# Second layer's attention stage: quartered low parts of the weight units computed by GpSimd instead of VectorE

## The reference, cut to what matters

```python
s = einsum('bnqhgd,bnkhd->bnhgqk', qb, kband) * dh ** -0.5     # 48 jobs: 4 token tiles x 12 heads
m = maximum(max(s), sink); p = exp(s - m)
p = p / (sum(p) + exp(sink - m))
o = einsum('bnhgqk,bnkhd->bqhd', p, vband)
mo = softmax(mq @ mk.T * dh ** -0.5) @ mv                       # 16 jobs: 4 tiles x 4 heads
mix = concatenate([o, mo]) @ w_out[l]
k, v = split(layer_norm(mem_2) @ w_mkv)                         # the second block's memory, for two layers
```

## Time and profile before

| | |
|---|---|
| median of 3 runs | 2278.38 us (2277.81 to 2281.79) |
| the profiled execution, its own time | 2280.4 us |
| its span | 2278.9 us |
| mean granted clock of TensorE | 0.958 |
| PE busy in the span | 2111.9 us (93%) |
| DVE busy | 1168.8 us (51%) |
| ACT busy | 883.9 us (39%) |
| POOL busy | 231.7 us (10%) |

### The profile page before, as it was taken

The page is one execution under the profiler, slowest core; times in us unless marked ns, Lnnn a source line. Parts: engine busy times, 40 slices in busy tenths (PEclk is TensorE's granted clock), DMA queues, the critical chain, the costliest instruction groups (busy, mean ns, idle before and its releaser), DMA issues.

```text
span 2278.9 us, 24588 instructions
## 1 busy us (share of the span) xinstructions
PE 2111.9 (93%) x9984; PEld 1716.7 (75%) x9984; DVE 1168.8 (51%) x2252; ACT 883.9 (39%) x1565; POOL 231.7 (10%) x155
## 2 busy tenths in 40 slices
PE   6998899999997999999999999999998899799787
PEld 6986688888786777788887878878776666577575
DVE  5325453333226666453332237998865248655553
ACT  5336443222124356442322222477451222456520
POOL 1000010000002000010000003766500000000000
PEclk9998599999998999999999999999999899999998
DMA  6330022233233212222222322322322312011211
GB/s 225 114 117 11 10 83 93 93 99 105 102 107 114 67 55 75 93 97 98 93 93 93 111 93 96 108 74 74 102 74 74 110 56 70 23 38 56 74 56 56
DMA packets 28800, 192.60 MB, mean 85 GB/s; under 512 B 3264, under 2 KB 3408, under 8 KB 7440
## 3 DMA queue, kind: packets, MB, share of 16 engines
q1 hardware_dynamic: 24848, 175.96, 22.5%
q0 software_dynamic: 3264, 12.99, 1.7%
q10 hardware_dynamic: 576, 2.10, 0.2%
HBM read 186.84 MB, written 4.19 MB: 84 GB/s over the span
## 4 chain that ended last, share of the span: by engine, by line
PE 77%; DVE 15%; ACT 6%; issue 1%; DMA 0%; POOL 0%; SPq 0%; DVEq 0%; POOLq 0%; ACTq 0%
PE bank L390 22%; PE bank L391 21%; PE bank L392 21%; DVE bank L1971 4%; PE bank L1660 2%; DVE WL L362 1%; PE bank L1551 1%; ACT WH L348 1%; PE bank L1090 1%; PE bank L1648 1%; PE bank L1099 1%; PE bank L1027 1%; PE bank L1561 1%; PE bank L2112 1%; PE bank L1653 1%
## 5 line engine op out<-in xcount | busy, mean ns | idle before, releaser
L390 PE MATMUL bank<-XH,WH 128*128 128x512 f32 (+1 forms) x1504 | 598.5, 398 | 25.4 <-DVE XL L551 10.3
L392 PE MATMUL bank<-XH,WL 128*128 128x512 f32 (+1 forms) x1504 | 568.5, 378 | 0.0
L391 PE MATMUL bank<-XL,WH 128*128 128x512 f32 (+1 forms) x1504 | 567.9, 378 | 0.0
L362 DVE TENSOR_TENSOR WL<-RAW,WH 128x2048 fp32r<-128x2048 f32 x128 | 293.2, 2291 | 462.8 <-ACT WH L348 462.8
L348 ACT ACTIVATE WH<-RAW 128x2048 fp32r<-128x2048 f32 x148 | 282.3, 1908 | 347.1 <-PE bank L392 341.7
L390 PEld LDWEIGHTS bank<-XH,WH 128*128 128x128 f32 x1504 | 286.8, 191 | 94.6 <-issue 24.7
L391 PEld LDWEIGHTS bank<-XL,WH 128*128 128x128 f32 x1504 | 287.1, 191 | 54.4 <-issue 5.6
L392 PEld LDWEIGHTS bank<-XH,WL 128*128 128x128 f32 x1504 | 286.3, 190 | 53.3 <-issue 0.6
L1971 DVE SCALAR_TENSOR_TENSOR bank<-conv_in,cols,bank 128x512 f32<-128x512 f32 x290 | 198.1, 747 | 1.1
L390 PE MATMUL bank<-WH,XH 128*128 128x512 f32 (+2 forms) x416 | 154.6, 372 | 9.8 <-DVE XL L551 6.3
L391 PE MATMUL bank<-WL,XH 128*128 128x512 f32 (+2 forms) x416 | 153.7, 369 | 0.0
(11 more groups left out here) (316 smaller groups left out, 3023.8 us busy)
## 6 DMA issues: line engine op xcount, KB each, us to landing
RAW<-weights SPq DMA_DIRECT2D x164, 1024.0 KB, 4.9
row_a<-rows POOLq DMA_DIRECT2D x7, 512.0 KB, 5.8
row_b<-rows POOLq DMA_DIRECT2D x6, 512.0 KB, 6.0
x_res<-x SPq DMA_DIRECT2D x1, 2048.0 KB, 16.7
kv<-mem_park POOLq DMA_DIRECT2D x2, 1024.0 KB, 5.1
out<-x_res ACTq DMA_DIRECT2D x4, 512.0 KB, 2.6
mem_tok<-mem SPq DMA_DIRECT2D x1, 1024.0 KB, 5.0
mem_tok<-mem POOLq DMA_DIRECT2D x1, 1024.0 KB, 8.4
```

What stands on the lines that cost most here:

```text
L362: dve.tensor_tensor(WL[j][:, :], RAW[j][:, :], WH[j][:, :].bitcast(F32), ALU.subtract).then_inc(*lo.mark())
L390: pe.matmul(ps, ah, bh, start=first, stop=False)
L391: pe.matmul(ps, ah, bl, start=False, stop=False)
L392: return pe.matmul(ps, al, bh, start=False, stop=last)
```

## The change

POOL gets a function `lower_quarter_pool`, with the body of `lower_quarter_dve` on the other engine, and `sliding_pool` runs the stage's 32 quarters in their order (`beside_pool`), with the four parking DMAs placed behind the last quarter of every second unit. `sliding_dve` issues no quarters. At the end of its stage DVE waits until U69 is lowered (`split_lo >= BESIDE_FIRST + 8`, which is 70). POOL begins with a wait for DVE's last lowering before the stage. `split_lo` counts in order, so each side waits for the other at the two seams.

```diff
+    def lower_quarter_pool(q):
+        u, j = lowered_pool[0], lowered_pool[0] % 2
+        s = slice(q * UNIT // 4, (q + 1) * UNIT // 4)
+        last = q == 3
+        if last:
+            POOL.wait_ge("split_hi", u + 1)
+        else:
+            POOL.wait_ge(*after("quarter", u, q))
+        part = pool.tensor_tensor(WL[j][:, s], RAW[j][:, s], WH[j][:, s].bitcast(F32), ALU.subtract)
+        part.then_inc(*(lo.mark() if last else G.mark()))
+        lowered_pool[0] += last
...
+    BESIDE_FIRST = U["mem2_kv", 0, 0] + 2
...
-    def beside_dve(e):
-        if e in QUARTERS:
-            lower_quarter_dve(QUARTERS[e])
-
-    def park_pool():
-        for layer in range(2):
-            POOL.wait_ge(*after("emptied", U["mem2_kv", layer, 1], 1))
-            pool.dma_start(mem_park[layer][:, 0:1024], m2_keys[:, :]).then_inc(*parked_keys.mark("park", layer, "keys", by=16))
-            POOL.wait_ge(*after("emptied", "mem2_v", layer, MEMT - 1))
-            pool.dma_start(mem_park[layer][:, 1024:2048], m2_values[:, :]).then_inc(*parked_values.mark("park", layer, "values", by=16))
+    def beside_pool():
+
+        lowered_pool[0] = BESIDE_FIRST
+        POOL.wait_ge("split_lo", BESIDE_FIRST)
+        for e in range(BESIDE_ENTRIES):
+            if e not in QUARTERS:
+                continue
+            lower_quarter_pool(QUARTERS[e])
+            if QUARTERS[e] == 3:
+                layer, unit = divmod(lowered_pool[0] - BESIDE_FIRST - 1, 4)
+                if unit == 1:
+                    POOL.wait_ge(*after("emptied", U["mem2_kv", layer, 1], 1))
+                    pool.dma_start(mem_park[layer][:, 0:1024], m2_keys[:, :]).then_inc(*parked_keys.mark("park", layer, "keys", by=16))
+                elif unit == 3:
+                    POOL.wait_ge(*after("emptied", "mem2_v", layer, MEMT - 1))
+                    pool.dma_start(mem_park[layer][:, 1024:2048], m2_values[:, :]).then_inc(
+                        *parked_values.mark("park", layer, "values", by=16))
+        lowered_pool[0] = U[A_SLOTS[2]]
...
-            for other in beside(n, BESIDE_LAGS[1]):
-                beside_dve(other)
             if n % 3 == 2 and n < 12:
                 rotate_dve(q_tok, SH - KB, ("q", 1), KB, ("q", 1), range(n // 3, n // 3 + 1), LATE_BLOCKS[0])
+        lowered[0] = BESIDE_FIRST + 8
+        DVE.wait_ge("split_lo", BESIDE_FIRST + 8)
...
-        park_pool()
+        beside_pool()
```

## The result

| | before | after |
|---|---|---|
| median of 13 runs each | 2277.81 us (2272.06 to 2281.79) | 2291.07 us (2280.92 to 2293.62) |
| ratio after / before | | 1.0055, 95% interval 1.0038 to 1.0072 |
| the profiled execution | 2280.4 us | 2293.11 us |
| its span | 2278.9 us | 2291.7 us |
| mean granted clock | 0.958 | 0.956 |

The account below looks back on a forecast made before the run. PE was taken to set the stage's pace. Stage -0.3 us (-0.3 - 0.3 + 0.3) and the seam summed to +0.6 us: 2281.0 for the profiled execution, median 2279.0, range 2276.5 to 2283.0.

Parts of the forecast that it names:

- Where PE waits for a quarter: At PE's starts of U64 and U67: POOL's later last quarters add 0.3 us and 0.0 or 0.1 us.
- DVE's held operations beside POOL: Stage's DVE operations with two SBUF inputs: line 1605 held at worst 1.29 us, within about 1.5 us slack; nothing charged.
- the wait of line 1607: PE's wait around 840 us for a small DVE operation behind a quarter: goes with the quarter, -0.3 us.
- rival B: Clock, at the stage's end: the new halt in the transposes delays full clock into the projection; +3.2 us, 2281.6, chance 0.15.
- The seam: Stage's end: DVE's wait for U69 delays the first XL; PE halts about 1 us, projection starts 942.5 against 941.88.
- A quarter on POOL: Each of 32 subtractions on POOL takes 1.29 us (bounds 1.16 and 1.74), starting 0.15 us behind ACT.
- DVE is relieved of 32 instructions: Over the stage, 32 quarters of 0.682 us leave DVE, 21.8 us, mostly beside PE's work.
- The loads of U71 and the parking DMAs: Around and after the stage's end: U71's load some 2 us later, parking DMAs behind quarters; nothing charged.
- Rival A: Seam costs nothing and DVE's relief reaches PE: -1.3 us, 2277.1; chance 0.2.
- The list of five waits: PE's waits behind DVE in the stage, 2.8 us together, claimed as all that relieving DVE could shorten.
- Rival C: Hold: each of 32 quarters delays line 1605 or 1602 past PE's slack, up to 0.46 us; +15 us, 2293; chance 0.05.

Follow-up runs that it names:

- e13: The change, with PE repeating eight transposes (0.9 us more work) 32 us ahead of U64; median 2277.10 us, ratio 0.9997.
- e5: The kernel before, unchanged, traced again with the stage's first job at 785.4 us; median 2273.59 us, ratio 0.9990.
- e10: The change with every unit's last quarter two entries earlier in the list, seam as in the change; median 2275.61 us, ratio 0.9992.
- e4: The change with DVE's wait for U69 moved behind the eight subtractions of the output projection's input; median 2289.80 us, ratio 1.0045.

## Why the prediction was wrong

**The step that failed is "Where PE waits for a quarter".** It costed the longer halt at U64 by its length, "+0.3 us". The length was right: 1.05 us after 0.78, and U67 0.5. What stands behind the halt was not costed: 37.5 us at half clock, 16.9 us, in the group that holds the traced execution. With it went a smaller term, DVE's held operations beside POOL, for which the text charged nothing: together with the wait of line 1607 that is gone they bring U64's start 0.3 us later, as much as the longer halt does, and by the table above each of the two alone goes with 13.6 us of half clock. The text did treat the clock, as rival B, but only for the new halt in the transposes, because the earlier trace rows showed half clocks there. Inside the stage showed 1.00 from start to end, and I took that as a property of the stage. It was one execution, with its halt of 0.78 us at a place where nothing followed. The rows were no evidence for a halt that is longer or stands elsewhere.

**The seam was mis-sized, +0.9 for 3.1 us.** POOL's chain (943.58 + 4.97 = 948.55) and DVE's first XL right behind it came as the text said. But the sum took the transposes at 6.67 us for 32, which is their time at half clock: the earlier trace rows cover the same stretch. At full clock the first four banks are full after 1.97 us instead of 3.33. PE had less work beside POOL's chain, and the halt grew from about 1 us to 2.5. The second 16 transposes then fell to half clock in part, 3.51 us in place of e13's 2.45, so 1.1 us of the 3.1 is clock again. e13 shows the other case: with the first 16 transposes at half clock (3.52 us) its halt there is 0.92 us, as forecast, and its seam 936.95 - 928.32 = 8.63 us, 2.4 more than e5's.

**What was right.** A quarter on POOL takes 1.28 us (forecast 1.29), and starts 0.08 us behind ACT's (850.46 + 0.61 = 851.07, start at 851.15; taken as 0.15). DVE is relieved of 32 instructions. It is busy 10 us less in all, not 22; 7.9 us of the difference are longer operations beside POOL (6.6 in line 1626, 1.3 in the rotation), the rest was not looked for. The loads of U71 and the parking DMAs cost nothing: from the projection to the end of the program the trace of after takes as long as that of before, 1337.4 against 1337.1 us.

**Rival A** (relief reaches PE) fell: at line 1134, which was 1122, the wait is 0.7 us instead of 0.3 (and none in e5); only the one of line 1607 is gone. The list of five waits, called all that relieving DVE could shorten, also left out PE's wait of 1.6 us for line 1231. **Rival B** was right in kind. At its own place it did happen, a half clock at 949 to 952.5, but that ended before the projection; the one that counts stood 95 us earlier. In e10 it did reach 4.3 us into the projection (932.3 to 939.3, projection from 935.04). **Rival C** gave 2293 us, which is nearly the measured time, by a mechanism that is not at work. The hold exists (below), but PE waits for it once, 0.66 us, not in every step, and e10 has all 32 quarters on POOL at no loss. A time that matches is no proof of its reason.

**The forecast beside the spread of the runs.** The text said that three runs lie 4 us apart and took 0.2% as what can be told. The kernel's runs lie in groups 5 to 15 us apart, and a change can move it from one set of groups to another without touching more than a microsecond of work. The range of 6.5 us was too narrow for that alone: e13 and the change differ by 14 us.

## What to carry to other kernels

Price a halt of the engine that sets the pace by what the clock does behind it, too: look for half clocks in several traces of the same kernel, and compare traces in which the stage begins at the same time, counting from its first job. When work moves to a slower engine, compute the slack of every single consumer and issue earlier what has none (here two entries earlier for one unit of eight gave back what the change had lost). Put a wait that only orders two engines behind the work that does not need it: e4's one moved line was worth 3.1 us.

## What the runs showed that I had not expected

**More work, less time, and the reverse.** 0.9 us of transposes took the change from some 2292 to 2277 us. The same work gave the kernel before executions of 2330 to 2346 us, six of 13, where none of 129 had been above 2302. Half a per cent between two versions of this kernel says little on the merit of either.

**The hold of DVE beside POOL.** The sum L1626, of one column with two SBUF inputs, took 0.15 us before, 0.159 at the longest. Now it takes up to 1.203 us. The 48 of them take 13.8 us in place of 7.2. The rotation is held as well; timeline of after:

```profile
814.54 1.41 POOL L395 TENSOR_TENSOR WL<-RAW,WH 128x512 fp32r<-128x512 f32 x1 [0.92 <-ACT WH L371]
814.74 1.37 DVE L1443 TENSOR_TENSOR q_tok<-q_tok,qT 128x128 f32<-128x128 f32 x1
...
816.55 0.44 PE L1039 MATMUL bank<-const,S 128*128 128x128 f32 x2 [0.66 <-DVE small L1134]
```

DVE starts 0.20 us behind POOL and ends 0.16 us behind it, in an operation that takes 0.28 us alone. The Trainium skill, in "SBUF — State Buffer", section "Who interferes with whom", says that the port pair which VectorE and GpSimd share is locked for a whole instruction. The traces agree, for operations of one column too: in the timeline of the halt at U64 above, L1626 ends at 852.43 and POOL's quarter at 852.41. The forecast that PE has slack for it held in the stage's 48 jobs. It failed at this one place, among the memory jobs, 0.66 us, and that wait is one of the two that move U64's start.
